# Narrow products of two blocks: three matmuls of 256 columns into one PSUM region, read there by their users

## What is computed

```python
# first block
p = rms_norm(x) @ w_in                       # 2048 -> 5 x 1024: b_gate, c_gate, v_a, val_b, gate_b
y_a = b_gate * conv3(c_gate * v_a)
y_b = silu(layer_norm(conv31(val_b * sigmoid(gate_b)) + bias))
x = x + rms_norm(concat(y_a, y_b) @ w_out)
x = x + rms_norm(square(relu(rms_norm(x) @ w_up)) @ w_down)     # 2048 -> 8192 -> 2048
# second block
u, gate = split(rmsnorm(x) @ w_in_a)         # 2048 -> 2 x 2048
x = x + ((window_means(u) - u) @ w_grp * scale * silu(gate)) @ w_out_a     # w_grp: 4 of 512 x 512
k, v = rope(rmsnorm(x) @ w_k), rmsnorm(x) @ w_v
q, gate = split(rmsnorm(x) @ w_in_b)         # 3 groups of 16 heads, gate
x = rmsnorm(x + (attention_of_3_dilations(rope(q), k, v) * silu(gate)) @ w_out_b)
```

## Time and profile before

| | |
|---|---|
| three executions | 2138.46, 2139.17, 2142.34 us; median 2139.17 |
| the profiled execution | 2139.48 us, of which span (first to last instruction) 2137.7 us |
| PE, matmuls | 2059.1 us busy (96%), 11160 |
| PE, weight loads | 1773.8 us busy (83%), 11160 |
| DVE | 1438.8 us busy (67%) |
| ACT | 964.0 us busy (45%) |
| DMA | 384 MB, 180 GB/s |
| granted TensorE clock, mean | 0.987 of 2.4 GHz |

### The profile page before, as it was taken

One profiled execution on the slowest core, in us unless ns is written; L12 is line 12 of the kernel. 1 busy time (PEld: TensorE's weight loads), 2 busy tenths in 40 slices (PEclk: granted clock), 3 DMA queues, 4 the chain that ended last, 5 costly groups with the idle time before them and its releaser, 6 DMA issues.

```text
span 2137.7 us, 27678 instructions
## 1 busy us (share of the span) xinstructions
PE 2059.1 (96%) x11160; PEld 1773.8 (83%) x11160; DVE 1438.8 (67%) x1845; ACT 964.0 (45%) x1226; POOL 8.0 (0%) x19
## 2 busy tenths in 40 slices
PE   6988899999999999999999998998999999999998
PEld 6877788888888888888879887778888888888886
DVE  5999774765556556555566766547845888888754
ACT  4433454544434444444445465434444454554542
POOL 0000000000000000000000000000000000000000
PEclk9999999999999999999999999999999999999999
DMA  6554456476566665656645565645666445545573
GB/s 221 168 157 145 142 193 221 145 237 192 185 197 188 187 194 181 197 189 188 194 140 179 175 197 160 222 126 192 205 191 194 155 153 167 166 151 166 159 265 109
DMA packets 305856, 384.21 MB, mean 180 GB/s; under 512 B 11673, under 2 KB 237209, under 8 KB 303936
## 3 DMA queue, kind: packets, MB, share of 16 engines
q1 hardware_dynamic: 305536, 382.22, 56.3%
q10 hardware_dynamic: 192, 0.23, 0.0%
HBM read 378.20 MB, written 4.19 MB: 179 GB/s over the span
## 4 chain that ended last, share of the span: by engine, by line
PE 83%; DVE 11%; issue 2%; ACT 2%; DMA 1%; SPq 0%; POOL 0%; DVEq 0%; POOLq 0%; ACTq 0%
PE job_banks L451 32%; PE job_banks L453 16%; PE job_banks L490 10%; PE job_banks L491 10%; PE job_banks L492 10%; DVE wide_rows L1154 4%; DVE weights_low L1071 4%; PE aux_banks L666 2%; DMA raw_weights<-in_w_in 1%; ACT weights_high L729 1%; DVE value L1087 1%; PE aux_banks L527 1%; PE aux_banks L492 0%; PE aux_banks L491 0%; PE aux_banks L490 0%
## 5 line engine op out<-in xcount | busy, mean ns | idle before, releaser
L1071 DVE TENSOR_TENSOR weights_low<-raw_weights,weights_high 128x1024 fp32r<-128x1024 f32 x696 | 841.8, 1223 | 526.6 <-ACT weights_high L729 524.9
L729 ACT ACTIVATE weights_high<-raw_weights 128x1024 fp32r<-128x1024 f32 x696 | 726.2, 1056 | 648.6 <-PE job_banks L492 283.1
L451 PE MATMUL job_banks<-act_a,weights_high 128*128 128x512 f32 (+1 forms) x2688 | 895.1, 388 | 35.6 <-DVE value L1087 16.9
L453 PE MATMUL job_banks<-act_a,weights_low 128*128 128x256 f32 (+1 forms) x2624 | 716.3, 274 | 0.0
L451 PEld LDWEIGHTS job_banks<-act_a,weights_high 128*128 128x128 f32 x2688 | 508.8, 191 | 141.6 <-DVE weights_low L1071 26.0
L453 PEld LDWEIGHTS job_banks<-act_a,weights_low 128*128 128x128 f32 x2624 | 504.2, 192 | 0.3
L451 PE MATMUL job_banks<-act_b,weights_high 128*128 128x512 f32 x1088 | 389.9, 402 | 7.0 <-DVE value L1087 7.0
L453 PE MATMUL job_banks<-act_b,weights_low 128*128 128x256 f32 x1088 | 304.6, 280 | 0.0
L451 PEld LDWEIGHTS job_banks<-act_b,weights_high 128*128 128x128 f32 x1088 | 205.5, 189 | 55.7 <-DVE weights_low L1071 8.1
L490 PE MATMUL job_banks<-weights_high,act_b 128*128 128x512 f32 x608 | 237.1, 390 | 0.0
L492 PE MATMUL job_banks<-weights_high,act_b 128*128 128x512 f32 x608 | 236.7, 389 | 0.0
(11 more groups left out here) (121 smaller groups left out, 1122.3 us busy)
## 6 DMA issues: line engine op xcount, KB each, us to landing
raw_weights<-in_w_up SPq DMA_DIRECT2D x128, 512.0 KB, 3.7
raw_weights<-in_w_down SPq DMA_DIRECT2D x128, 512.0 KB, 4.4
raw_weights<-in_w_in_b SPq DMA_DIRECT2D x128, 512.0 KB, 4.2
raw_weights<-in_w_in SPq DMA_DIRECT2D x80, 512.0 KB, 3.6
raw_weights<-in_w_in_a SPq DMA_DIRECT2D x64, 512.0 KB, 4.5
raw_weights<-in_w_out SPq DMA_DIRECT2D x32, 512.0 KB, 4.7
raw_weights<-in_w_out_a SPq DMA_DIRECT2D x32, 512.0 KB, 4.1
raw_weights<-in_w_k SPq DMA_DIRECT2D x32, 512.0 KB, 4.6
```

The source lines that it names most:

```text
L451: made = e.matmul(o_both, wh[:, k, cols], rhs, start=opens, stop=False)
L453: made = e.matmul(o[:, 0, low_toks], wl[:, k, cols], x[:, first + kt, 0, low_toks], start=False, stop=kt == job.tiles - 1)
L729: e.activation(high[:, s, :], raw[:, r, :], ACT.Copy).then_inc(*high_done.inc(n))
L1071: e.tensor_tensor(low[:, s, :], raw[:, r, :], high[:, s, :].bitcast(F32), ALU.subtract).then_inc(*low_done.inc(n))
```

## The change

A narrow job that does not run by half uses one bank: 256 tokens for `f` = 0 in its first half, for `f` = 1 in its second. `narrow_unit` issues three matmuls of 256 columns into that region where it issued one of 512 and one of 256. The four banks are taken one by one, so that a narrow job comes back to a bank after four, and each job's `freed` names the operation that reads the bank last (the tanh, the product, the rotation). `part` and `gather` are left out for these jobs, and ACT and DVE read the bank (`of_job`, `there`). In `take_up` ACT makes the Relu from PSUM into `value` and DVE squares it, for all 32 jobs. The eight jobs by half keep both banks, `part` and `gather`; in `half_unit` the two matmuls of the high weights now stand ahead of the two of the low ones. Wide jobs stay as they are.

```diff
@@ build
+        for first in (mix_b, up[0], pool_u, keys):
+            for job in first[0:2]:
+                job.by_half = True
...
-            if job.pair < 2:
-                job.before = in_pair[job.pair] if job not in ended else None
-                if job not in begun:
-                    in_pair[job.pair] = job
-            job.freed = taken if job.wide else gathered
+            if job.wide or job.by_half:
+                taken_banks = [2 * job.pair, 2 * job.pair + 1]
+            else:
+                job.bank = 2 * job.pair + (turns - 1) // 2 % 2
+                taken_banks = [job.bank]
+            job.before = [in_bank[bank] for bank in taken_banks]
...
+            frees(mix_b[2 * i], squashed, ("gate_b", i))
+            frees(mix_b[2 * i + 1], g_made, i)
...
+        for g in range(N_POOL):
+            for i, job in enumerate(grp[g]):
+                frees(job, product, ("grp", g, i))
...
+        def of_job(job):
+            if job.by_half:
+                return value_of(job)
+            return banks[:, job.bank, :].rearrange("p (f n) -> p f n", f=2)
+
+        def there(e, job):
+            e.wait_ge(*(gathered.at((job.id, 0)) if job.by_half else unit_used.at(job.last)))
@@ tensor
+            def narrow_unit(job, buf, first, u, comes):
...
+                e.wait_ge(*low_done.at(n))
+                if u == 0:
+                    bank_free(job, 0)
+                for k in range(job.per_unit):
...
+                    xh, xl = x[:, first + kt, 0, :], x[:, first + kt, 1, :]
+                    for f in range(2):
+                        cols = slice(f * P, (f + 1) * P)
+                        e.matmul(o[:, f, :], wh[:, k, cols], xh, start=kt == 0 and f == 0, stop=False)
+                        e.matmul(o[:, f, :], wh[:, k, cols], xl, start=False, stop=False)
+                        made = e.matmul(o[:, f, :], wl[:, k, cols], xh, start=False,
+                                        stop=kt == job.tiles - 1 and f == 1)
+                made.then_inc(*unit_used.inc(n))
@@ scalar
-                part(c_job)
-                e.wait_ge(*gathered.at((c_job.id, 0)))
+                there(e, c_job)
...
-                e.activation(cvpad[:, :, CONV_A - 1:], value_of(c_job), ACT.Copy).then_inc(*kept.inc(("c", i)))
+                e.activation(cvpad[:, :, CONV_A - 1:], of_job(c_job), ACT.Copy).then_inc(*kept.inc(("c", i)))
...
-                part(job)
+                if job.by_half:
+                    part(job)
+                there(e, job)
...
+                e.activation(value_of(job), of_job(job), ACT.Relu).then_inc(*kept.inc(("relu", s, c)))
@@ vector
-                gather(job)
+                if job.by_half:
+                    gather(job)
                 v = value_of(job)
-                e.wait_ge(*gathered.at((job.id, 0)))
-                e.scalar_tensor_tensor(v, v, 0.0, v, ALU.max, ALU.mult).then_inc(*product.inc(("z", s, c)))
+                e.wait_ge(*kept.at(("relu", s, c)))
+                e.tensor_tensor(v, v, v, ALU.mult).then_inc(*product.inc(("z", s, c)))
...
-                    gather(job)
                     v, k = value_of(job), g * tiles_g + 2 * i
-                    e.wait_ge(*gathered.at((job.id, 0)))
+                    there(e, job)
+                    value_there(job.pair)
                     e.wait_ge(*gate_scaled.at(k + 1))
-                    e.tensor_tensor(v, v, silu_gate[:, k:k + 2, :], ALU.mult).then_inc(*product.inc(("grp", g, i)))
+                    e.tensor_tensor(v, of_job(job), silu_gate[:, k:k + 2, :], ALU.mult).then_inc(
+                        *product.inc(("grp", g, i)))
```

More of the change, by code:

```diff
@@ L131, in __init__ @@
         self.count = len(self.units)
-        self.id = self.at = self.last = self.pair = self.before = self.freed = None
+        self.by_half = False
+        self.id = self.at = self.last = self.pair = self.bank = self.before = self.freed = None
 def build(nc, t, out):
@@ L439, in narrow_unit @@
                         x_there(comes(first + kt, h))
+                    opens = kt == 0 and halves[0] == 0
                     for f in range(2):
                         bank = 2 * job.pair + f
[L442 to L445, removed]
+                        if opens:
+                            bank_free(job, f)
                         o = banks[:, bank, :].rearrange("p (a n) -> p a n", a=2)
[L447 to L454, removed]
+                        made = e.matmul(o[:, :, toks], wh[:, k, f * P:(f + 1) * P], x[:, first + kt, :, toks],
+                                        start=opens, stop=False)
+                    for f in range(2 if low_halves else 0):
+                        o = banks[:, 2 * job.pair + f, :].rearrange("p (a n) -> p a n", a=2)
+                        made = e.matmul(o[:, 0, low_toks], wl[:, k, f * P:(f + 1) * P], x[:, first + kt, 0, low_toks],
+                                        start=False, stop=kt == job.tiles - 1)
                 if halves[-1] == 1:
@@ L459, in narrow @@
                 for u in range(job.count):
-                    narrow_unit(job, buf, first, u, BOTH, BOTH, comes)
+                    narrow_unit(job, buf, first, u, comes)
                     aside.step()
@@ L465, in narrow_by_half @@
                     for u in range(job.count):
-                        narrow_unit(job, buf, 0, u, (0,), () if u >= job.count - LATE else (0,), comes)
+                        half_unit(job, buf, 0, u, (0,), () if u >= job.count - LATE else (0,), comes)
                 between()
@@ L481, in wide_unit @@
                 toks = slice(half * P, (half + 1) * P)
-                if opens and u == 0 and job.before is not None:
-                    e.wait_ge(*job.before.freed.at((job.before.id, half)))
+                if opens and u == 0:
+                    bank_free(job, half)
                 if half == 0:
@@ L819, in scalar @@
                 units_of(gate)
-                part(gate)
-                e.wait_ge(*gathered.at((gate.id, 0)))
+                if gate.by_half:
+                    part(gate)
+                there(e, gate)
                 if i:
@@ L981, in scalar @@
                 units_of(keys[i])
-                part(keys[i])
                 part_free[keys[i].pair] = (rotated, ("key", i))
@@ L1038, in scalar @@
                     aside.step()
-                part(job)
-                e.wait_ge(*gathered.at((job.id, 0)))
-                e.activation(part_of(job), value_of(job), ACT.Tanh, scale=0.5).then_inc(*squashed.inc(("gate", i)))
+                there(e, job)
+                part_there(job.pair)
+                e.activation(part_of(job), of_job(job), ACT.Tanh, scale=0.5).then_inc(*squashed.inc(("gate", i)))
                 e.wait_ge(*product.at(("gate", i)))
@@ L1414, in rotate @@
             def rotate(event, job, dst):
[L1415 to L1416 removed]
+                v, part = of_job(job), part_of(job)
+                there(e, job)
                 e.tensor_tensor(part, v, cos, ALU.mult).then_inc(*rotated.inc((event, "cos")))
```

129 lines of the change are left out of this document (80 added, 49 removed).

## The result

In 12 runs of each, the changed kernel took 2144.3 us (median; 2142.66 to 2146.79) and the kernel before 2140.13: the ratio is 1.0021, with a 95% interval from 1.0012 to 1.0030. One of the twelve of the kernel before took 11624.05 us, for no cause that is on record, and the ratio is taken without it. The forecast was 2147, slower: 7.8 us more than before, where 4.5 were measured. The small number is the rest of two large ones: some 21 us lost to the matmuls, some 17 gained where VectorE (DVE) or a wait for the sum had set the pace.

The account below looks back on a forecast made before the run. PE was taken as the bound nearly everywhere, DVE in the convolution (58 to 223.2 us). +23.2 - 8.2 - 1.9 - 3.9 - 1.4 = +7.8 us gave 2147 us; the forecast case's own range was 2140 to 2154, the wider 2120 to 2160.

Parts of the forecast that it names:

- The matmul's price, +23.2 us: Where PE is the bound, 2792 pairs go from 0.3517 to 0.3600 us each as three matmuls: +23.2 us.
- a matmul with its load costs its columns and some 13 ns, whatever its length: Price rule for PE's matmuls: a third matmul adds 13 ns, so three of 256 columns take 0.360 us.
- the lower bound of 0.3405: Least time in us for three matmuls, if 256 columns took half of 512 in a wide product: -31 us over 2792 pairs.
- the first rival: Narrow products where PE is the bound: load hidden, three matmuls in 0.357 us or less; at 0.117 each, 2122 us; chance 0.25.
- Convolution, -8.2: From 58 to 231 us: DVE stays the bound and loses 12 sums of 0.683 us, so its end comes 8.2 us earlier.
- PE's waits for banks turn into waits for split weights: During the convolution, PE would wait for split weights in place of banks; no separate size given.
- 231 to 299 us, -1.9: PE's two waits for a sum in this stretch, 1.9 us together, go away.
- Group products, -5.6 and +1.7: From 1312 to 1343 us: next product opens 5.6 us earlier, half clock after PE's wait costs 1.7; together -3.9 us.
- Gates, -1.4: At 1979.54 us PE's wait for a head behind a gate job loses a sum and ACT's wait: -1.4 us.
- The second: DVE's 8.2 us unseen in the convolution, or PE loses its clock more often; +23.2 alone is 2162 us; chance 0.12.
- The third: The second load of the same weights is left out, three matmuls take 0.3467 us, kernel 2110 us; chance 0.03.
- the fourth: Something no row shows, such as a slower read of PSUM beside PE's writes; no size given; chance 0.03.

Follow-up runs that it names:

- experiment 1: The kernel before, with only its matmul of 512 columns cut into two of 256; banks, copy and sum unchanged: 2158.61 us, ratio 1.0098.
- experiments 4 to 7: The changed kernel with one (192, then 128 columns), two or all three (192) narrow matmuls shortened, leaving out work; one execution each: 2115.5, 2115.1, 2093.2, 2077.8 us.
- experiment 2: The changed kernel with an unused DVE pass of 512 elements put back at the old sum's place in each of 108 jobs: 2156.97 us, ratio 1.0088.
- experiment 8: The changed kernel with three matmuls and no sum only in mixer, group products and first two gates, the old pair and sum elsewhere: 2124.89 us, ratio 0.9931.
- experiment 9: The kernel with the new scheme only in mixer, group products and first two gates, its pairs regrouped as 512, 512, 256, 256: 2115.70 us, ratio 0.9886.

## Why the prediction was right, point by point

The direction and the size of both sides were right; their difference came out at a little over half of the 7.8 us forecast, with a loss 1.6 us smaller and gains 2.6 us larger by the profiles.

- **What bounds the kernel.** Right. In the stages between 299 and 1118 us nothing that DVE or ACT lost was seen, but for the start of up stage 0 (below), and every ns of a matmul was.
- **The matmul's price, +23.2 us.** Measured +21.6 in experiment 1. The three took 0.3600 as taken from the earlier trace rows, and an up stage 46.1 as said. Three smaller items lie inside. Between 231 and 299 us experiment 1 has 168 pairs that cost nothing (-0.13 from the convolution's end to the first wide product): PE's waits for the sum there shrink from 1.9 to 0.8 us instead. In up stage 0 its 192 pairs should cost 1.3 us (0.0067 each) and the stage is 3.1 longer; the other 1.8 is the clock, below. And the clock gives as much back in the gates. Behind the wait of the earlier trace rows the kernel before has 3.4 us at half the clock, which experiment 1 has not (table by stage of the kernel before, then the timeline of experiment 1):

```profile
1980.00:1984.00 4.00, 4.00 (x21) 3.81 (x21) 2.80 (x6) 0.71 (x2) 0.00 (x0) 0.57 0.74 231
```

```profile
2000.69 2.25 PE L670 MATMUL aux_banks<-resid,scratch 128*128 128x128 f32 x18 [2.44 <-issue]
```

  The same 18 matmuls took 3.34 us before, 1.1 more, and the two pairs behind them 0.6 more: 1.7 us. So the matmuls alone cost 21.6 - 1.8 + 1.7 = 21.5 us over 2624 pairs, 0.0082 each, which from 0.3600 leaves 0.3518 for the old pair, 0.3517 said. The share of a quarter at 0.3467 stands too: of the last 1152 pairs from 1499.9 us on, 624 lie in stretches at 0.346 to 0.347, while the up stages are at 0.353.
- **"a matmul with its load costs its columns and some 13 ns, whatever its length".** Wrong: at 192 and 128 columns some 0.110 us is paid, more than columns and 13 ns, and by my reading it is the load (experiments 4 to 7). The lower bound of 0.3405, half a wide matmul, was reached only with less work, and the first rival's 0.117 was not there; the pair's short second step was the difference of two starts, and the matmul before it had paid for it.
- **Convolution, -8.2.** Exact: -8.22 at its end, one sum left on DVE between 58 and 230 us where there were 13. What I said of PE was wrong in kind: "PE's waits for banks turn into waits for split weights" did not come. Behind the first jobs it waited for them once, 1.0 us up to 182.84, then ran on to 207.50 and stood for 15.1 us in one piece:

```profile
207.50 0.28 PE L494 MATMUL job_banks<-act_a,weights_low 128*128 128x256 f32 x1
222.88 1.19 PE L619 MATMUL aux_banks<-wide_rows,early_tables 128*128 128x256 f32 x2 [15.11 <-DVE wide_rows L1228]
```

- **231 to 299 us, -1.9.** Measured -1.34 (-9.56 after -8.22): PE is busy 68.0 of 68 us now, and the 168 pairs, whose 1.4 us my first term had already, are paid in it.
- **Group products, -5.6 and +1.7.** A circle was to take 3.47 us, and the wide product behind them to start 5.6 us earlier. From the split on ACT that opens the stage (1309.87 before, 1309.25 after) to the wide product it is 33.32 us before and 27.56 after, 5.76 less. In experiment 1 it is 33.32 again (1320.91 to 1354.23), with three matmuls for each pair: PE's price doesn't count there, the sum does. Six circles last 20.84 us, 3.47 each, and the product waited 4.6 us (4.7 said); its first matmuls run at half the clock:

```profile
1315.24 0.68 DVE L1458 TENSOR_TENSOR value<-job_banks,wide_rows 128x512 f32<-128x512 f32 x1
...
1336.08 0.68 DVE L1458 TENSOR_TENSOR value<-job_banks,wide_rows 128x512 f32<-128x512 f32 x1
```

```profile
1331.91 0.28 PE L494 MATMUL job_banks<-act_b,weights_low 128*128 128x256 f32 x1
1336.81 0.80 PE L558 MATMUL job_banks<-weights_high,act_a 128*128 128x512 f32 x1 [4.62 <-DVE value L1458]
1337.41 0.63 PE L559 MATMUL job_banks<-weights_low,act_a 128*128 128x512 f32 x1
```

  The lead falls from 6.38 to 4.96 over that wide stage, so the clock took 1.4 us, 1.7 said; the six pairs' worth behind that figure came from no row, and that it was near is luck. That it is the clock shows over the runs: from the first matmul of this wide product to the keys it is 91.6 us before and in experiment 1, at a clock of 1.00 throughout; 93.0 in the changed kernel, 93.5 in experiments 2 and 8, and 94.4 in experiment 9, where 3.0, 4.0 to 4.1 and 5.9 us of it ran at half the clock, a little under half of that time in each. The first 4 us of it in the changed kernel and in experiment 1:

```profile
1336.81:1340.81 4.00, 4.00 (x11) 3.26 (x12) 2.52 (x3) 2.11 (x3) 0.00 (x0) 0.62 0.76 256
```

```profile
1354.23:1358.23 4.00, 4.00 (x18) 3.31 (x19) 3.05 (x4) 2.07 (x3) 0.00 (x0) 1.00 0.82 254
```

- **Gates, -1.4.** Too small: the queries and gates cost 4.9 us after the change and 7.6 in experiment 1, so -2.7. The wait of 2.64 us, which experiment 1 still has with 2.4, is gone whole. I had taken off one sum and one wait and kept the rest of the wait; which further step of the chain became shorter I have not traced. Against the kernel before it is more: the 1.7 us of half clock behind the wait, which I had left out, are gone too, some 4.3 us in all.
- **Left out: the start of up stage 0.** PE waits there for ACT (1.4 to 2.2 us) and then works at a lower clock for some us. How long differs between the runs. Table by stage, experiment 1, then the changed kernel:

```profile
395.00:400.00 5.00, 2.83 (x23) 2.69 (x22) 3.52 (x6) 2.12 (x4) 0.10 (x1) 0.91 0.75 225
400.00:405.00 5.00, 5.00 (x26) 5.00 (x25) 3.05 (x6) 2.71 (x8) 1.00 (x2) 0.50 0.72 240
405.00:410.00 5.00, 5.00 (x41) 5.00 (x41) 2.74 (x4) 0.56 (x2) 0.00 (x0) 0.90 0.01 2
```

```profile
385.00:390.00 5.00, 3.62 (x32) 3.41 (x30) 3.48 (x6) 1.79 (x4) 0.46 (x1) 1.00 0.91 277
390.00:395.00 5.00, 5.00 (x32) 5.00 (x32) 3.39 (x7) 2.71 (x8) 0.64 (x2) 0.66 0.64 218
395.00:400.00 5.00, 4.80 (x42) 4.59 (x42) 3.94 (x7) 2.07 (x4) 0.00 (x0) 1.00 0.00 0
```

  A granted clock of 0.50 is 1.2 GHz. The kernel before has one stretch at 0.66 too; experiment 8 stays at 1.00, and its up stage 0 is 1.5 us shorter than before with the same matmuls (100.1 against 101.5). This stage makes 2.1 us of the 18.0 between experiment 1 and the changed kernel. The changed kernel and experiment 8 have the same wait there, 1.38 us, and only the first loses its clock; what decides that stays open. That it is the clock alone is my reading; no run took it by itself.
- **The rivals.** The faster one failed on 0.1200. The second (gains given back) failed on -8.22 and by experiment 2, which shows each gain where DVE was unloaded. The third failed on the loads, one to each matmul. Of the fourth nothing is seen: an up stage is 46.07 us with the users reading PSUM and without.

The account of the gains (experiment 1 to the changed kernel, from the table): -8.3 to the convolution's end, -1.2 to the first wide product, -2.1 in up stage 0, 0 in the other up stages, -5.8 by the group products, +1.4 for the clock behind them, +0.7 in the keys (where the changed kernel has 10.2 us at half the clock and experiment 1 has 6.8), -2.7 in queries and gates: -18.0. Predicted were 15.4.

## What to carry to other kernels

Where a change trades one engine's work against another's, price it by stage: here the matmul counted wherever PE decides and the sum in the few stages where DVE does, and the version that used each form only where its engine decided was worth 0.7%, where the change as a whole was a loss of 0.2%. To split a matmul cost 13 ns here beside a pair at 0.3467 and 7 beside one at 0.3532, and a matmul with its own weight load got no cheaper from 192 columns to 128 (by the estimate above, from some 230 down). Take the price of a matmul from start to start over many steps, never from one step between neighbours of different length.

## What the runs showed that was not expected

- The order of 512, 256, 512, 256 costs 5 ns a pair against 512, 512, 256, 256 (0.3532 and 0.3483, up stages of 45.21 and 44.58 us); the whole kernel took 0.34% less in the second order. Runs of eight give no more (0.3489).
- A matmul with its load has a floor of 0.109 to 0.112 us: 128 columns cost what 192 do (0.3488 and 0.3489 for the three).
- The stall of PE before the convolution's end grew from 7.7 to 15.1 us while the kernel's step there came 8.2 us earlier: a longer wait of an engine that isn't the bound is a sign of slack; what it can cost is the clock behind it, as the 1.4 us behind the wait of 4.6.
